# A convolution stage reordered: its matrices built on GpSimd, its layer norm placed behind the next tiles, tanh in place of sigmoid

## What is computed

```python
x = x + 0.5 * swiglu(rmsnorm(x, g1), w1_in, w1_out)
h = rmsnorm(x, g2)
u_conv, q, k, v, g_conv, g_attn = split(h @ w_in)
a, g = split(u_conv, 2)
z = a * sigmoid(g)                       # GLU, 1024 channels
z = causal_depthwise_conv(z, width=31) + dw_bias
a = silu(layernorm(z)) @ conv_w_proj
b = sliding_window_attention(q, k, v) @ attn_w_o
x = x + (sigmoid(g_conv) * a + sigmoid(g_attn) * b) @ w_out
x = x + 0.5 * swiglu(rmsnorm(x, g3), w2_in, w2_out)
```

## Time and profile before

| quantity | value |
|---|---|
| median of three runs | 3516.7 us (lowest 3510.5) |
| profiled execution | 3507.7 us |
| its span, slowest core | 3505.7 us |
| spans of all cores | 3489.9 to 3505.7 us |
| PE busy | 3076.8 us (88%) |
| DVE, ACT, POOL busy | 1326.2, 846.8, 551.9 us |
| convolution stage, first GLU product to the end of its last layer norm | 982.0 to 1722.1 us |
| attention stage, up to the second feed-forward | 1722.1 to 2605.8 us |

### The profile page before, as it was taken

How to read it: one execution, slowest core, us unless ns; L and a number is a source line. 1 busy time by engine, 2 the same in 40 slices (tenths; PEclk the granted TensorE clock), 3 DMA queues, 4 the chain that set the end, 5 groups by cost and what they waited for, 6 DMA issues and landing times.

```text
span 3505.7 us, 42706 instructions; the slowest of 8 cores (3489.9 to 3505.7 us)
## 1 busy us (share of the span) xinstructions
PE 3076.8 (88%) x15172; PEld 1394.6 (40%) x15172; DVE 1326.2 (38%) x1699; ACT 846.8 (24%) x1362; POOL 551.9 (16%) x565
## 2 busy tenths in 40 slices
PE   4999999999979797974477888887869999999998
PEld 2444444444434453532233333333324444444444
DVE  3323355333452826350533443333323233332333
ACT  3111132111222222231264444544210111111110
POOL 2001021000110000010053445433400000000000
PEclk9999999999989898987789999999989999999999
DMA  6518886331566473859413443236762124921202
GB/s 163 79 21 113 106 191 149 55 52 19 138 167 167 129 214 88 242 132 184 123 37 116 125 132 81 94 114 156 207 177 47 20 44 78 230 58 19 45 1 96
DMA packets 307597, 386.61 MB, mean 110 GB/s; under 512 B 199744, under 2 KB 199744, under 8 KB 307264
## 3 DMA queue, kind: packets, MB, share of 16 engines
q1 hardware_dynamic: 274704, 286.33, 28.7%
q0 software_dynamic: 32688, 97.56, 18.4%
HBM read 326.18 MB, written 119.54 MB: 127 GB/s over the span
## 4 chain that ended last, share of the span: by engine, by line
PE 75%; DMA 8%; SPq 5%; DVE 5%; ACT 3%; issue 2%; POOL 2%; DVEq 0%; ACTq 0%; POOLq 0%
PE ps L349 75%; SPq L377 2%; SPq L375 2%; DMA zsh<-zfm 2%; DMA x_59<-x 1%; DVE y L666 1%; DMA EB<-eb 1%; DVE y L664 1%; DMA sg_156<-sig_s 1%; POOL mg L783 1%; DMA x_52<-x 1%; DVE qn L715 1%; DMA toep_105<-toepb 1%; ACT rs_190 L363 1%; ACT rs_189 L363 0%
## 5 line engine op out<-in xcount | busy, mean ns | idle before, releaser
L363 ACT ACTIVATE tfA_96<-ps 128x512 f32<-128x512 f32 x88 | 52.5, 597 | 581.4 <-PE ps L349 572.0
L645 DVE TENSOR_TENSOR y<-ps,cbias 128x512 f32<-128x512 f32 x64 | 45.8, 725 | 322.9 <-PE ps L349 322.8
L363 ACT ACTIVATE tfA_98<-ps 128x512 f32<-128x512 f32 x88 | 52.5, 596 | 356.9 <-PE ps L349 356.8
L363 ACT ACTIVATE tfA_99<-ps 128x512 f32<-128x512 f32 x88 | 52.5, 597 | 284.8 <-PE ps L349 284.7
L363 ACT ACTIVATE tfA_97<-ps 128x512 f32<-128x512 f32 x88 | 52.5, 597 | 237.6 <-PE ps L349 237.4
L743 POOL TENSOR_TENSOR pt_166<-et_162,EB 128x1024 bf16<-128x1024 bf16 x31 | 66.4, 2142 | 208.1 <-ACT et_162 L363 208.0
L363 ACT ACTIVATE et_162<-ps 128x1024 bf16<-128x1024 f32 x63 | 64.3, 1021 | 75.4 <-PE ps L349 74.7
L349 PE MATMUL ps<-hB_109,wB_117 128*128 128x512 bf16 x64 | 20.0, 471 | 70.2 <-DVE zfm L614 70.2
L743 POOL TENSOR_TENSOR pt_164<-et_162,EB 128x1024 bf16<-128x1024 bf16 x32 | 68.5, 2140 | 71.1 <-ACT et_162 L363 71.0
L743 POOL TENSOR_TENSOR pt_167<-et_163,EB 128x1024 bf16<-128x1024 bf16 x31 | 66.3, 2140 | 83.9 <-ACT et_163 L363 83.5
L363 ACT ACTIVATE et_163<-ps 128x1024 bf16<-128x1024 f32 x63 | 64.0, 1015 | 50.3 <-PE ps L349 50.2
(11 more groups left out here) (670 smaller groups left out, 7003.0 us busy)
## 6 DMA issues: line engine op xcount, KB each, us to landing
toep_105<-toepb SPq DMA_DIRECT2D x22, 640.0 KB, 5.7
toep_106<-toepb SPq DMA_DIRECT2D x21, 640.0 KB, 5.4
toep_107<-toepb SPq DMA_DIRECT2D x21, 640.0 KB, 5.4
toepb<-toep POOLq DMA_DIRECT2D x16, 640.0 KB, 24.4
zsh<-zfm SPq DMA_DIRECT2D x256, 32.0 KB, 2.1
sg_156<-sig_s SPq DMA_DIRECT2D x22, 256.0 KB, 3.7
xM_153<-x SPq DMA_DIRECT2D x11, 512.0 KB, 5.3
xM_154<-x SPq DMA_DIRECT2D x11, 512.0 KB, 4.9
```

The source lines that it names most:

```text
L363: P.add("act", lambda e: e.activation(**kw), reads, writes, 0.21 + n / 1200.0 + (0.3 if accum is not None else 0.0), table=TABLE.get(func))
L645: dve(lambda e, b=b, yv=yv, G=G: e.tensor_tensor(out=yv.ap, in0=ps[:, b, :].rearrange("p (g r c) -> p g r c", g=4, r=8), in1=cbias.t[:, 64 ...
```

## The change

The block matrices are no longer passed, converted and loaded. Only their distinct values are: kk, 128 x 2560, one value for each partition, group, lag block and offset; and cmask, 128 x 16, which is 1 where the channel of the partition equals the column. Each round POOL multiplies the two, both broadcast, to build each of the 16 matrices (2560 elements per partition) into one of the three toep buffers, with a planner price of 5.7.

In program order a round is now: GLU of both tiles, layer norm of the round before, then 16 steps, each with two gate products and one convolution group. The last layer norm stands after qkv(0). tfB has six buffers in place of eight, and begins 2 KB earlier. Of the wB weights only the GLU half is loaded ahead; the gate half is issued during glu(0), wQ during the gates of round 3, wM during qkv(0), wO during qkv(1), each issue after a given product.

Sigmoid(g) is written as (tanh(g/2) + 1)/2: the +1 goes into the multiplications (a scalar_tensor_tensor in place of a tensor_tensor), the factor 2 on z is taken up by a doubled bias and 4 EPS in the layer norm, the one on the gates by 0.5 in outp. `TABLE` puts Tanh with Silu.

```diff
-TABLE = {AF.Silu: "silu", AF.Sigmoid: "sig", AF.Exp: "nl", AF.Ln: "nl"}
+TABLE = {AF.Silu: "silu", AF.Tanh: "silu", AF.Exp: "nl", AF.Ln: "nl"}
-    tfB = [buf("tfB%d" % i, 182 + 2 * i, [T], F32) for i in range(8)]
+    tfB = [buf("tfB%d" % i, 180 + 2 * i, [T], F32) for i in range(6)]
+    kk = buf("kk_t", 192, [64 * 40], BF16)
+    cmask = buf("cmask_t", 197, [16], BF16)
-    for j in range(16):
-        dma("pool", "tp%d" % (j % 4), toepb_d[:, j * 2560:(j + 1) * 2560], toep_d[:, j * 2560:(j + 1) * 2560], [], [("toepb", j)],
-            128 * 2560 * 6, after=[mark[0]])
-    for j in range(16):
+    for j in range(8):
         dma("pool", "wB%d" % j, wB[j].v().ap, wb_d[j].rearrange("p (k n) -> p k n", n=256), [], [wB[j].v()], 128 * 2048 * 4)
+    dma("pool", "c6", kk.v().ap, kk_d, [], [kk.v()], 128 * 2560 * 4)
...
     def glu(t):
...
+            if t == 0:
+                dma("pool", "wB%d" % (8 + c), wB[8 + c].v().ap, wb_d[8 + c].rearrange("p (k n) -> p k n", n=256), [], [wB[8 + c].v()],
+                    128 * 2048 * 4, after=[m_])
-            act(tf.v(), PS(bg), AF.Sigmoid, T)
+            act(tf.v(), PS(bg), AF.Tanh, T, scale=0.5)
...
+    def conv_part(G):
+        tp = toepr.next()
+        pool(lambda e, tp=tp, G=G: e.tensor_tensor(
+            out=tp.t[:].rearrange("p g b (q c) -> p (g b q) c", c=16),
+            in0=kk.t[:, 160 * G:160 * G + 160].rearrange("p (a o) -> p a o", o=1).to_broadcast([128, 160, 16]),
+            in1=cmask.t[:].rearrange("p (o c) -> p o c", o=1).to_broadcast([128, 160, 16]), op=ALU.mult),
+            [kk.v(), cmask.v()], [tp.v()], 5.7)
...
+    def gates_conv(u):
         for G in range(16):
+            t = 2 * u + G // 8
+            gate(t, G % 8, 0)
+            m_ = gate(t, G % 8, 1)
+            conv_part(G)
+            if u == 3 and G < 12 and G % 2 == 0:
+                load_wq(G // 2, [m_])
...
     for u in range(4):
         glu(2 * u)
         glu(2 * u + 1)
-        gates(2 * u)
-        gates(2 * u + 1)
-        conv(u)
-        lnorm(u)
+        if u:
+            lnorm(u - 1)
+        gates_conv(u)
...
+            if t == 0 and j < 8:
+                dma("pool", "wB%d" % (8 + j), wM[j].v().ap, wm_d[j].rearrange("p (k n) -> p k n", n=256), [], [wM[j].v()],
+                    128 * 2048 * 4, after=[m_])
+            if t == 1 and j < 4:
+                dma("pool", "wO%d" % j, wO[j].v().ap, wo_d[j].rearrange("p (k n) -> p k n", n=D), [], [wO[j].v()],
+                    128 * 2048 * 4, after=[m_])
...
     for t in range(NT):
         qkv(t)
+        if t == 0:
+            lnorm(3)
+            bcast_row("c0", gC, g3_d)
         att(t)
```

More of the change, by code:

```diff
@@ L237, in build @@
     wo_d = din("wo", [4, 128, 2048])
-    toep_d = din("toep", [128, 64 * 640])
+    kk_d = din("kk", [128, 64 * 40])
+    cmask_d = din("cmask", [128, 16])
     eb_d = din("eb", [128, 4096])
@@ L255, in build @@
     sig_d = scr("sig_s", [NT, 16, 128, 512], F32)
-    toepb_d = scr("toepb", [128, 64 * 640], BF16)
     base = (nc.sbuf_base + 63) // 64 * 64
@@ L621, in glu, with gate @@
                     dma("sp", "z%d" % (g % 8), dv.ap, zfm.t[16 * gg:16 * gg + 16, c, :, :], [zfm.v(c)], [dv], 128 * 128 * 2 * 2)
-    def gates(t):
+    def gate(t, c, j):
         h = hB[t % 2]
[L625 to L633, removed]
@@ L635, in conv @@
-    def conv(u):
-        for G in range(16):
[L637 to L648, removed]
+        b = bankB.next()
@@ new lines, in gate @@
+        m_ = mm([PS(b)], [(ps[:, b, :], wB[8 + c].t[:, kc, 128 * j:128 * j + 128], h.t[:, kc, :], kc == 0, kc == KC - 1)
+                     for kc in range(KC)], [wB[8 + c].v(), h.v()], KC * 0.2158)
+        k = tfBr.n % 6
+        tf = tfBr.next()
+        act(tf.v(), PS(b), AF.Tanh, T, scale=0.5)
+        dma("sp", "sg%d" % k, sig_d[t, 2 * c + j], tf.t[:], [tf.v()], [("sig", t, 2 * c + j)], 128 * T * 4)
+        return m_
+    def conv_part(G):
[5 more added lines that the diff above has]
+            [kk.v(), cmask.v()], [tp.v()], 5.7)
+        b = bankC.next()
+        mm([PS(b)], [(ps[:, b, gi * 128:gi * 128 + 128], zsh.t[:, 4 * G + gi, 4 - j:132 - j], tp.t[:, gi, j, :], j == 0, j == 4)
+                     for gi in range(4) for j in range(5)], [tp.v(), zsh.v(slice(4 * G, 4 * G + 4))], 20 * 0.058)
+        yv = y.v(slice(None), slice(64 * G, 64 * G + 64), f=lambda a: a.rearrange("p r (g c) -> p g r c", g=4))
+        dve(lambda e, b=b, yv=yv, G=G: e.tensor_tensor(
+            out=yv.ap, in0=ps[:, b, :].rearrange("p (g r c) -> p g r c", g=4, r=8),
+            in1=cbias.t[:, 64 * G:64 * G + 64].rearrange("p (g o c) -> p g o c", g=4, o=1).to_broadcast([128, 4, 8, 16]), op=ALU.add),
+            [PS(b), cbias.v()], [yv], T)
@@ L779, in merge @@
                 s_ = sgs[j]
-                dve(lambda e, b=b, s_=s_: e.tensor_tensor(out=s_.t[:], in0=ps[:, b, :], in1=s_.t[:], op=ALU.mult),
-                    [PS(b), s_.v()], [s_.v()], T)
+                dve(lambda e, b=b, s_=s_: e.scalar_tensor_tensor(out=s_.t[:], in0=s_.t[:], scalar=1.0, in1=ps[:, b, :],
+                                                                 op0=ALU.add, op1=ALU.mult), [PS(b), s_.v()], [s_.v()], T)
             mv = mg.v(fc)
@@ L871, in lay_out @@
     dk = a["conv_dw_kernel"]
-    toep = np.zeros((16, 8, 64, 5, 8, 16), np.float32)
+    lags = np.zeros((16, 8, 64, 5, 8), np.float32)
     kc = dk.reshape(CW, 64, 16)
@@ L879, in lay_out @@
                     for c in range(16):
-                        toep[c, r, :, b, q, c] = kc[CW - 1 - lag, :, c]
+                        lags[c, r, :, b, q] = kc[CW - 1 - lag, :, c]
     eb = np.full((128, 2, 2, 2, 4, 128), -1e4, np.float32)
```

31 lines of the change are left out of this document (14 added, 17 removed).

## The result

The changed kernel takes 3383.2 us (median of four runs, 3377.1 to 3410.8), against 3513.2 for the kernel before on the same chip (median of three; a fourth execution, 3800.1 us, fell into a slower state and is left out): a ratio of 0.9645 (of the means), interval 0.9577 to 0.9712. 3370 was forecast. Its profiled execution took 3379.6 us with a span of 3378.1, so 128 us less than the execution read for the prediction; 138 were forecast.

A forecast was written before the change was run, and what follows sets the result against it. Convolution stage, 740 us: PE floor 512, loss 228. Forecast 512 + 20 + 45 + 0 + 15 + 10 = 602, gain 138, so 3507.7 us becomes 3370 (chance 0.60), range 3295 to 3480.

The forecast's parts named there:

- start: Start of the convolution stage, where PE lost about 26 us: 20 us of loss kept, bounds 10 and 26.
- DVE's lag, three rounds: GLU of rounds 1 to 3: DVE, given layer norm between products, falls behind PE; 15 us each, 45 together, bounds 0 and 90.
- builds: Matrix builds on POOL in the gate stretches: 5.35 us each, free up to 5.7 us; loss 0 to 33, taken as 0.
- last layer norm and hM of tile 1: Around qkv: 15 us lost to the last layer norm (0 to 34), 10 to the hM transpose (0 to 43).
- 11.6 x 2.28: In the lag: DVE time for GLU products at 2.28 us over the 11.6 steps into which the planner packs the layer norm.
- rival A: Convolution and attention stages: the DVE lag does not matter, gain 208 us, 3300 us; chance 0.14.
- matrices' traffic: Conversion and 64 loads of the matrices go; PE's 25.2 us wait for them counted inside the convolution stage's 228 us loss.
- burst of weights: Last round: attention-stage weight loads beside a 43.35 us hM transpose; spreading them was counted as removing it and PE's wait there.
- Tanh: Tanh for sigmoid in the convolution stage: costs nothing, table loads fall from 11 to about four, gaining only at the start.
- rival D: On ACT, Tanh is not in Silu's table: extra table loads, 0 to 30 us in all, about 3385 us; chance 0.05.
- Rival B: DVE and POOL lock each other: six builds a round hold up DVE, 32 us a round, 3466 us; chance 0.13.
- Rival C: A build takes 10.7 us; above 5.7 each microsecond costs 52 us, loss 260 us, 3630 us; chance 0.08.

The follow-up runs named there:

- e3: Changed kernel with the block matrices converted and loaded by DMA again, POOL building nothing: ratio 0.9881 to the kernel before, 3462.8 us.
- e1: Changed kernel with the layer norms of rounds 0 to 2 put ahead of the next two GLU tiles again: 0.9734 of the kernel before, 3414.0 us.
- e7: Changed kernel with the last round's layer norm and the broadcast of gC moved ahead of qkv(0): 0.9633 of the kernel before, 3385.2 us.
- e6: Changed kernel with sigmoid in place of tanh and the factors taken back: 0.9634 of the kernel before, 3380.2 us.
- e2: Changed kernel with wQ, wM and wO loaded in one burst behind the four rounds: 0.9665 of the kernel before, 3376.4 us.
- e5: Changed kernel with the planner's price for the GLU product raised from 0.69 to 2.05 us: 0.9614 of the kernel before, 3372.0 us.
- e10: Changed kernel plus an idle 640 KB load into SBUF per group, EB loaded behind round 3: 0.9786 of the kernel before, 3433.5 us.
- e4: Changed kernel with each block matrix built twice in the same buffer: 1.0176 of the kernel before, 3567.5 us.
- e12: Changed kernel in the old order (all gates, all convolution groups, then the round's own layer norm), matrices still built: 0.9731 of the kernel before, 3416.8 us.

## Why the prediction was right, and where its reasons were not

| term of the sum, us | forecast | measured |
|---|---|---|
| floor of the rounds | 512 | not a row: 512 |
| start | 20 | 20.7 (8 channel steps in 48.35 us instead of 27.6; 14 to 21 over the cores) |
| DVE's lag, three rounds | 45 | 25.9 |
| builds | 0 | 0 |
| not forecast, in the rounds | - | 26.5 |
| last layer norm and hM of tile 1 | 25 | 28.6 |
| sum | 602 | 614 |

From the first GLU product to the last copy of zsh the changed kernel takes 585.1 us; of this 26.5 remain besides the three terms named. The last term is 25 plus the 3.6 us by which the way from there to the first output product (179.4 us; before 185.1, with 34.3 bare) exceeds what the forecast left of it, 175.8. So by this sum some 12 us fewer were gained than forecast (by the executions 10). That the point came out so close is in part luck: the lag cost 19 us less than forecast, and 26.5 us were not forecast at all.

Taken out of the changed kernel one at a time, the parts cost, by the profiled executions: the builds 83 us (e3), the place of the layer norms of rounds 0 to 2 34 (e1), that of the last one 6 (e7), tanh 1 (e6), the weights in turn nothing (e2); the last three lie within the scatter of the runs. Together that is some 120 of the 128 us, so the gain is in the main the builds and the order. In the old order the shares can differ.

*The lag* was mis-sized. The step that failed is 11.6 x 2.28: beside scalings the product takes 2.02 to 2.05 us, and 11.6 x 2.03 + 33.9 - 40.0 - 5.2 is 12, not 15; with the first halves of four rows' statistics (some 3 us) done ahead of these steps, at 1093 to 1096 us, some 9, and 8.6 a round were measured (25.9 over three). That the order matters, e1 shows (30 us). That the lag comes from the planner's wrong price, as the prediction said against rival A, e5 bears out: with the true price the waits for zfm fall from 25.9 to 1.4 us. What the prediction left out is the price of the cure: the layer norm, spread to the end of GLU, runs into the next builds and is locked out there, 11 us a round (e5).

*What was not forecast:* some 3 us in each of rounds 1 and 2, and 16 in round 3, 5.8 of them waits for gate buffers and 3.4 for zsh, at a mean clock of 0.98 instead of 1.00; another 3.5 are no loss, but a first step of the attention stage that stands in round 3. The waits for gate buffers are a rest of what rows 5 showed.

*The matrices' traffic* is the term that the prediction left without a price of its own. It put 25.2 us on it, the waits that name it, inside the 228. Put back into the changed kernel the traffic costs 83 us (e3), and bytes that nobody waits for cost 54 (e10). The number survived because the sum was built up from PE's floor, in which the cause of a loss that goes is not asked. Its reason for the 43 us transpose, the burst of weights, fits the trace of before, and no run separates the two there; e3 and e10 show that the matrices' bytes can lengthen that transpose too (16 to 31 and 13 to 35 us over the cores). How the 97 us that round 3 lost before divide between burst, traffic and layer norm stays open.

*The last layer norm* came close by two errors: of its 34 us only some 10 are hidden (e7), so some 24 are left where 15 were forecast, and PE waits 3.4 us for the hM of tile 1 where 10 were. *Tanh* behaved as forecast (e6). Of rival D, nothing is left: none of the three table loads stands between Tanh and Silu. (The Trainium skill, "ScalarE: Activation LUTs", section "Table sets: the hidden batching unit", lists no such set; here the trace decides.) *Rival B* did not happen in the changed kernel, where the scalings are done before the builds of the next groups start (none in the rounds takes over 1.5 us), but its mechanism is real: e5 shows the DVE held up by POOL, the case that no row of before showed, by three builds a round and not six. (The Trainium skill, "SBUF — State Buffer", section "Who interferes with whom", states an exclusive lock for a pair like this; the trace agrees, with 5.3 to 5.5 us for a scaling of 1.28, three times a round.) *Rival C* had the right price line (e4); *rival A* falls with the 25.9 us of waits for zfm and with e1.

Of what was to show it, the length of the stage, the small waits and the absence of a tfB wait above 15 us came; a build took less than my lower bound.

## What to carry to other kernels

Waits that name a transfer are not its price: bytes that nobody waits for can hold up the stores and transposes beside them (e10), so read the DMA share of the stretch and what stands behind the slow transfer in its queue. And look which transfers were in flight beside it: a run that moves a suspect away from the place of the loss, as e2 does, neither convicts nor clears it. Put a block of work beside the stretch that leaves its engine free (layer norm under gates, as e12 does by chance), and not beside long POOL operations that hold it up (e5). An order made of e12's first rounds and the changed kernel's last one suggests itself from the losses; it was not tried, nor was the true price with builds held back until the layer norm is done.

## What the hardware showed unexpectedly

- A POOL product of 2560 bf16 elements with both inputs broadcast takes 4.49 us (1.75 ns an element), less than the line through the earlier trace rows gives.
- A DVE scaling of 1.28 us beside a POOL build of 4.49 us takes 5.3 to 5.5 us (e5).
- At 258 GB/s the DMA engines are 94% busy and PE falls behind (e10). A transposed load that takes 7 to 11 us over the cores of the changed kernel takes 16 to 31 with loads of matrices and weights beside it (e3), 13 to 35 with idle loads (e10), and 22 to 43 before, with six loads of weights.
